# The end of a feed-forward stage in another order, and a fifth landing buffer for weights

## What is computed

```python
def first_block(x, ...):
    for l in range(DEPTH):                                  # DEPTH = 2
        x = layer_norm(ALPHA * x + 0.5 * swiglu(x, ffn1_w13[l], ffn1_w2[l]), ...)
        m = mixer(x, w_in[l], ...)
        x = layer_norm(ALPHA * x + m, ...)
        x = layer_norm(ALPHA * x + 0.5 * swiglu(x, ffn2_w13[l], ffn2_w2[l]), ...)

def second_block(x, ...):
    for layer in range(DEPTH):
        h = swiglu_2(rms_norm(x, g[0]), ffn_w_in[layer, 0], ffn_w_out[layer, 0])
        x = x + 0.5 * rms_norm(h, g[1])
        h = token_mixer(rms_norm(x, g[2]), mix_w_in[layer], ...)
        x = x + rms_norm(h, g[3])
        h = swiglu_2(rms_norm(x, g[4]), ffn_w_in[layer, 1], ffn_w_out[layer, 1])
        x = x + 0.5 * rms_norm(h, g[5])

def swiglu(x, w13, w2):
    a, b = jnp.split(x @ w13, 2, axis=-1)                   # 2816 hidden features each
    return (jax.nn.silu(a) * b) @ w2
```

## Time and profile before

| | us |
|---|---|
| median of 3 runs (lowest, highest) | 2115.8 (2115.5, 2116.16) |
| profiled execution, its time | 2114.63 |
| its span in the profile | 2112.9 |
| TensorE busy with matmuls | 2090.4 (99%) |
| VectorE busy | 1686.0 (80%) |
| ScalarE busy | 1081.8 (51%) |
| POOL busy | 84.5 (4%) |
| SyncE's transfers, share of 16 DMA engines | 57.6% |
| issue to landing, median, by kind of weight load | 3.2 to 4.1 |
| TensorE's granted clock, mean | 0.999 |

### The profile page before, as it was taken

One profiled execution on the slowest core, in us unless ns is written; L12 is line 12 of the kernel. 1 busy time (PEld: TensorE's weight loads), 2 busy tenths in 40 slices (PEclk: granted clock), 3 DMA queues, 4 the chain that ended last, 5 costly groups with the idle time before them and its releaser, 6 DMA issues.

```text
span 2112.9 us, 28855 instructions
## 1 busy us (share of the span) xinstructions
PE 2090.4 (99%) x10552; PEld 1774.3 (84%) x10552; DVE 1686.0 (80%) x3158; ACT 1081.8 (51%) x1568; POOL 84.5 (4%) x127
## 2 busy tenths in 40 slices
PE   8999999999999999999999999999999999999998
PEld 7887999888788799988878887988888888888886
DVE  6888766888888877778888887779888888678886
ACT  6445554544544455444454446575445445665543
POOL 0000010000000000000000001010000000101000
PEclk9999999999999999999999999999999999999999
DMA  7765755566566574656646666346665765645663
GB/s 249 234 194 169 224 166 157 188 217 191 174 218 196 174 234 139 190 168 224 196 153 213 215 191 196 125 136 207 214 195 171 220 196 163 185 140 165 214 191 98
DMA packets 314368, 395.56 MB, mean 187 GB/s; under 512 B 17972, under 2 KB 272212, under 8 KB 313972
## 3 DMA queue, kind: packets, MB, share of 16 engines
q1 hardware_dynamic: 309120, 375.52, 57.6%
q0 software_dynamic: 4944, 18.14, 2.7%
q10 hardware_dynamic: 164, 0.06, 0.0%
HBM read 392.59 MB, written 1.06 MB: 186 GB/s over the span
## 4 chain that ended last, share of the span: by engine, by line
PE 93%; DVE 4%; ACT 1%; issue 1%; DMA 1%; POOL 0%; SPq 0%; DVEq 0%; POOLq 0%; ACTq 0%
PE bank L309 25%; PE bank L311 25%; PE bank L310 25%; PE bank L303 4%; PE bank L304 4%; PE bank L305 4%; DVE w_lo L293 1%; PE bank L478 1%; DVE hidden L464 1%; PE bank L1442 1%; PE bank L1463 1%; PE bank L972 1%; DMA stage<-in_mix_w_in 1%; PE bank L1534 1%; ACT w_hi L286 0%
## 5 line engine op out<-in xcount | busy, mean ns | idle before, releaser
L286 ACT ACTIVATE w_hi<-stage 128x1024 fp32r<-128x1024 f32 x711 | 747.1, 1058 | 635.0 <-PE bank L311 527.2
L293 DVE TENSOR_TENSOR w_lo<-stage,w_hi 128x1024 fp32r<-128x1024 f32 x711 | 865.2, 1224 | 213.7 <-ACT w_hi L286 206.9
L309 PE MATMUL bank<-w_hi,xt_hi 128*128 128x512 f32 x1760 | 692.9, 394 | 0.6 <-DVE xt_lo L816 0.4
L311 PE MATMUL bank<-w_hi,xt_lo 128*128 128x512 f32 x1760 | 686.7, 390 | 0.0
L310 PE MATMUL bank<-w_lo,xt_hi 128*128 128x512 f32 x1760 | 686.5, 390 | 0.0
L464 DVE STREAM_TRANSPOSE hidden<-hidden 32x128 f32<-32x128 f32 (+1 forms) x1376 | 391.7, 285 | 21.3
L309 PEld LDWEIGHTS bank<-w_hi,xt_hi 128*128 128x128 f32 x1760 | 331.0, 188 | 69.6 <-issue 1.2
L311 PEld LDWEIGHTS bank<-w_hi,xt_lo 128*128 128x128 f32 x1760 | 330.9, 188 | 68.8
L310 PEld LDWEIGHTS bank<-w_lo,xt_hi 128*128 128x128 f32 x1760 | 331.1, 188 | 66.5
L309 PE MATMUL bank<-w_hi,mt_hi 128*128 128x512 f32 x768 | 304.1, 396 | 6.7 <-DVE mt_lo L546 6.7
L311 PE MATMUL bank<-w_hi,mt_lo 128*128 128x512 f32 x768 | 299.8, 390 | 0.0
(11 more groups left out here) (275 smaller groups left out, 1384.2 us busy)
## 6 DMA issues: line engine op xcount, KB each, us to landing
stage<-in_ffn_w SPq DMA_DIRECT2D x352, 256.0 KB, 3.2
stage<-in_ffn_w_in SPq DMA_DIRECT2D x352, 256.0 KB, 3.2
stage<-in_ffn_w SPq DMA_DIRECT2D x88, 512.0 KB, 3.7
stage<-in_ffn_w_out SPq DMA_DIRECT2D x88, 512.0 KB, 3.7
stage<-in_w_in SPq DMA_DIRECT2D x80, 512.0 KB, 4.1
stage<-in_mix_w_in SPq DMA_DIRECT2D x56, 512.0 KB, 3.9
stage<-in_w_out SPq DMA_DIRECT2D x16, 512.0 KB, 4.1
stage<-in_mix_w_out SPq DMA_DIRECT2D x16, 512.0 KB, 3.4
```

What stands on the lines that cost most here:

```text
L286: act.activation(w_hi[:, u % RING, :], stage[:, u % STAGED, :], ACT.Copy).then_inc(S["hi_ready"], 1)
L293: dve.tensor_tensor(w_lo[:, u % RING, :], stage[:, u % STAGED, :], f32(w_hi[:, u % RING, :]), ALU.subtract).then_inc(S["lo_ready"], 1)
L309: pe.matmul(o, m_hi, hi, start=first, stop=False)
L311: return pe.matmul(o, m_lo, hi, start=False, stop=last)
```

## The change

Three things are changed. The number of landing buffers goes from 4 to 5, so that a load waits for the low part of the unit five back. The memory for it comes from two row tables that are given up: `ones8` and `g_neg1` now lie in `gm`, and POOL writes the ones anew in each of the second block's mixers; the steps of the lower bounds count on `tables_out` in place of a semaphore of their own. And the end of each feed-forward stage has another order on VectorE, in the first block on ScalarE too.

```diff
-STAGED = 4
+STAGED = 5
...
-    margins=6, mixrows2=32, wg_in=16, wg_hi=1, wg_lo=1,
+    margins=7, mixrows2=32, wg_in=16, wg_hi=1, wg_lo=1,
...
-        g_neg1 = sb("g_neg1", [2 * H, T])
-        ones8 = sb("ones8", [2 * H, T])
...
+        ones8 = gm[0:2 * H, 1, 0:T]
-        g_neg_rows = hidden_flat[0:2 * H, 768:768 + T], g_neg1[:, :]
+        g_neg_rows = hidden_flat[0:2 * H, 768:768 + T], gm[0:2 * H, 0, 0:T]
...
+            if s < BLOCK2:
+                act_silu(act, s, 1, STEPS - 1)
             act_norm_sq(act, s, 0)
-            act_silu(act, s, 1, STEPS - 1)
+            if s >= BLOCK2:
+                act_silu(act, s, 1, STEPS - 1)
             act_h(act, s, 1, STEPS - 1)
...
-            dve_norm_start(dve, s, 0)
-            dve_gate(dve, s, 1, STEPS - 1)
+            dve_norm_start(dve, s, 0, lambda: dve_gate(dve, s, 1, STEPS - 1))
             dve_norm_var(dve, s, 0)
+            dve_h(dve, s, 1, STEPS - 1)
             dve_norm_x(dve, s, 0)
-            dve_h(dve, s, 1, STEPS - 1)
...
-        def dve_norm_start(dve, s, t):
+        def dve_norm_start(dve, s, t, between=lambda: None):
+
             wait_acc(dve, s, t)
...
                    .then_inc(S["ln_mean"], 1)
+                between()
                 dve.wait_ge(S["ln_mean"], ln_at(s, t))
...
                     dve.tensor_tensor(r[:, t, c], acc[:, t, c], rows[:, 0, c], ALU.mult).then_inc(S["post_scaled"], 1)
+                between()
...
-            act.wait_ge(S["lb_step"], 3)
-            act.activation(lb_tmp[:, 3:5, :], lb_tmp[:, 1:3, :], ACT.Exp).then_inc(S["lb_step"], 1)
+            act.wait_ge(S["tables_out"], 6)
+            act.activation(lb_tmp[:, 3:5, :], lb_tmp[:, 1:3, :], ACT.Exp).then_inc(S["tables_out"], 1)
...
                 dve.wait_ge(S["g_rows"], at("g_rows", L))
+                dve.wait_ge(S["margins"], at("margins", L, 1))
...
+            pool.memset(ones8, 1.0).then_inc(S["margins"], 1)
             pool.memset(xp[:, :, 0:2], 0.0).then_inc(S["margins"], 1)
...
-            pool.memset(ones8[:, :], 1.0).then_inc(S["ones_set"], 1)
...
-            dve.wait_ge(S["ones_set"], 2)
```

More of the change, by code:

```diff
@@ L857, in dve_tables @@
             mx = lb_tmp[:, 0, :]
-            dve.tensor_tensor(mx, lbr_tab[:, 0, :], lbr_tab[:, 1, :], ALU.max).then_inc(S["lb_step"], 1)
-            dve.wait_ge(S["lb_step"], 1)
+            dve.tensor_tensor(mx, lbr_tab[:, 0, :], lbr_tab[:, 1, :], ALU.max).then_inc(S["tables_out"], 1)
+            dve.wait_ge(S["tables_out"], 4)
             for l in range(2):
-                dve.tensor_tensor(lb_tmp[:, 1 + l, :], lbr_tab[:, l, :], mx, ALU.subtract).then_inc(S["lb_step"], 1)
+                dve.tensor_tensor(lb_tmp[:, 1 + l, :], lbr_tab[:, l, :], mx, ALU.subtract).then_inc(S["tables_out"], 1)
         def dve_lower_bounds(dve):
             mx, e = lb_tmp[:, 0, :], lb_tmp[:, 3:5, :]
[L865 to L874, removed]
+            dve.wait_ge(S["tables_out"], 7)
+            dve.tensor_tensor(lb_tmp[:, 5, :], e[:, 0, :], e[:, 1, :], ALU.add).then_inc(S["tables_out"], 1)
+            dve.wait_ge(S["tables_out"], 8)
+            dve.reciprocal(mx, lb_tmp[:, 5, :]).then_inc(S["tables_out"], 1)
+            dve.wait_ge(S["tables_out"], 9)
+            dve.tensor_tensor(lb_tab[:, 1, :], e[:, 1, :], mx, ALU.mult).then_inc(S["tables_out"], 1)
+            dve.memset(lb_tab[:, 0, :], 0.0).then_inc(S["tables_out"], 1)
+            dve.wait_ge(S["tables_out"], 11)
+            dve.tensor_scalar(om_tab, lb_tab, -1.0, 1.0, ALU.mult, ALU.add).then_inc(S["tables_out"], 1)
+            dve.wait_ge(S["tables_out"], 12)
         def w_cols(w, c0, n, k0=0, nk=KD):
@@ L1792, in gate_rows @@
                 dve.wait_ge(S["g_rows"], at("g_rows", L))
+                dve.wait_ge(S["margins"], at("margins", L, 1))
                 rev = (slice(None), slice(None, None, -1))
-                dve.tensor_tensor_scan(g_cum_rows[0], ones8[:, :], g_lf_row, 0.0, ALU.mult, ALU.add)\
+                dve.tensor_tensor_scan(g_cum_rows[0], ones8, g_lf_row, 0.0, ALU.mult, ALU.add)\
                    .then_inc(S["g_scan"], 1)
-                dve.tensor_tensor_scan(g_cum_rows[1][rev], ones8[:, :], g_lf_row[rev], 0.0, ALU.mult, ALU.add)\
+                dve.tensor_tensor_scan(g_cum_rows[1][rev], ones8, g_lf_row[rev], 0.0, ALU.mult, ALU.add)\
                    .then_inc(S["g_scan"], 1)
@@ L1808, in gate_bounds @@
                     dve.wait_ge(S["g_scan"], at("g_scan", L, d + 3))
-                    dve.tensor_tensor_scan(o, ones8[:, :], a, -1e30, ALU.mult, ALU.max).then_inc(S["g_scan"], 1)
+                    dve.tensor_tensor_scan(o, ones8, a, -1e30, ALU.mult, ALU.max).then_inc(S["g_scan"], 1)
                 for d in range(2):
@@ L1981, in pool_mix2 @@
             pool.memset(va[:, :, :, P:P + 1], 1.0).then_inc(S["margins"], 1)
-            pool.wait_ge(S["margins"], at("margins", L, 3))
+            pool.wait_ge(S["margins"], at("margins", L, 4))
             pool.memset(q_odd_parts[1][0:64], 0.0).then_inc(S["margins"], 1)
-            pool.wait_ge(S["margins"], at("margins", L, 4))
+            pool.wait_ge(S["margins"], at("margins", L, 5))
             pool.wait_ge(S["x_turned"], xt_at(s, 1, 1))
             pool.memset(aqk_t[64:P, 0:4, :], 0.0).then_inc(S["margins"], 1)
-            pool.wait_ge(S["margins"], at("margins", L, 5))
+            pool.wait_ge(S["margins"], at("margins", L, 6))
             pool.wait_ge(S["rot"], at("rot", L))
```

4 lines of the change are left out of this document (2 added, 2 removed).

## The result

The changed kernel takes 2111.8 us (median of 16 runs, 2111.19 to 2112.9), the kernel before 2115.74 (16 runs, 2114.86 to 2116.42): ratio 0.9981, interval 0.9975 to 0.9987. That is 3.9 us less, and the forecast of 2111.7 is met within 0.1. The profiled execution took 2112.07 (span 2110.3).

What follows compares the result with a forecast made beforehand. TensorE, busy 99%, was taken as the bound, losing time mainly at eight feed-forward ends. Terms 2.9 - 0.1 + 1.1 + 0.2 = 4.1 us off the median 2115.8 gave 2111.7, range 2109.0 to 2114.5.

Steps and rivals of the forecast that it cites:

- The place of the loss: TensorE's stalls at the ends of all eight feed-forward stages, 10.7 us, most of what there is to win.
- Block 1, 3 x 0.93: Three first-block ends gain 0.93 us each from the new order, after a new wait for xt_lo.
- 1.64: TensorE's loss in us at one first-block feed-forward end: 0.65 at the transposes plus 0.99 at the low part.
- 0.71: Part in us of a first-block end's 1.64 that turns into a new wait for xt_lo at the next opening.
- The end before block 2, +0.07: Fourth first-block end, where VectorE's chain counts: normalisation 0.27 later, low part's 0.34 gone from behind it, gain 0.07 us.
- The other three of block 2, -0.03 each: Second-block ends but the last: VectorE's chain 0.03 us later each, -0.1 together; the wait only moves.
- The last end, 1.13: Program's last feed-forward end: no next stage, so the low part's wait goes and 1.13 us come off.
- The order in sum: The reordering's terms in the forecast sum: 2.9 in block 1, -0.1 in block 2, 1.1 at the last end.
- The fifth buffer, 0.2: Earlier loads save only TensorE's 0.2 us wait for the copy at line 1618.
- the upper bound that was given with it: Fifth buffer worth at most 1 us, if small waits at the program's start go too.
- the first rival: Buffer worth more: a twentieth of ScalarE's 51 us of landing waits counts, 2.5 us, giving 2109.2; chance 0.12.
- POOL beside the low part: POOL's rstd running beside VectorE's low part on their shared port: counted as nothing, bound 2.9 us at seven ends.

Runs made afterwards that it cites:

- experiment 3: Kernel before with SiLU and gate product moved first in block 1, low part still last, four buffers: 2120.25 us, ratio 1.0018.
- experiment 4: Kernel before with only the low part moved ahead of the normalisation, SiLU still late, four buffers: 2113.12 us, ratio 0.9986.
- Experiment 5: Changed kernel with tile 0's xt_lo put between VectorE's two weight subtractions: 2107.73 us, ratio 0.996 to the kernel before.
- experiment 1: Kernel before with the new order alone, four landing buffers and the old tables: 2112.85 us, ratio 0.9986.
- experiment 12: Kernel before profiled a second time without any edit: 2116.12 us.
- experiment 11: The kernel of experiment 3 profiled a second time: 2121.25 us.
- experiment 8: Experiment 1 with the lower bounds' work 18 units later, four buffers: 2112.02 us, ratio 0.998 to the kernel before.
- experiment 6: Experiment 5 with one weight subtraction behind tile 1's normalisation at three block-1 openings: 2106.98 us, ratio 0.9958 to the kernel before.
- experiment 9: Experiment 6 with the lower bounds moved as in experiment 8, five buffers: 2107.06 us, ratio 0.9957 to the kernel before.

## Why the prediction was right, and where it was not

- *The place of the loss: right.* Eight ends, two stalls each in block 1, one in block 2. With the low part put first the waits for it vanish at all eight, and experiments 3 and 4 take the two moves apart.
- *Block 1, 3 x 0.93: measured 0.88, 0.77 and 0.82.* The path was the forecast one (normalisation, two halves, two subtractions, xt_lo), each step within 0.07. The sum left out that the matmul behind a wait is followed late: at the opening 194.69, then 195.03, 0.34 apart instead of 0.23. The old stalls had such steps too (0.31 behind the one at 191.23), and these go with them. So at the first end 1.77 is gone where 1.64 was counted, and 0.90 comes back where 0.71 was counted: 0.87 against 0.93. Experiment 5 shows that this wait is the subtractions' doing.
- *The end before block 2, +0.07: measured -0.07. The other three of block 2, -0.03 each: measured -0.15, -0.11 and -0.16.* The mis-sized term is the step from the normalisation to the product with the gain, which the earlier trace rows gave as 1.20 because the low part stood between them. In the new order the product follows at once and waits for the normalisation's end, 1.31 behind its start:

```profile
1275.55 1.28 DVE L780 SCALAR_TENSOR_TENSOR x<-r,rstd,x 128x1024 f32<-128x1024 f32 x1
1276.86 1.29 DVE L805 TENSOR_TENSOR xh<-x,rows 128x512 f32<-128x512 f32 x2
...
1280.34 1.28 DVE L820 TENSOR_TENSOR xt_lo<-bank,xt_hi 128x512 fp32r<-128x512 f32 x2
...
1281.08 0.50 PE L308 MATMUL bank<-w_hi,xt_hi 128*128 128x512 f32 x1 [0.83 <-DVE xt_lo L820]
```

- *The last end, 1.13: measured 1.24.* Nothing comes back here, and the stall goes together with the late restart behind it (0.31 instead of 0.23).
- *The order in sum: forecast 3.9, in the profiles 2.47 - 0.07 - 0.42 + 1.24 = 3.2, in medians 3.0.*
- *The fifth buffer, 0.2: measured 1.0.* This term was wrong: the measurement is the upper bound that was given with it, and not for the reason given there. The 0.2 was read as one wait for line 1618, which the buffer removes. Right in kind: in the changed kernel it is gone. But it comes and goes without the buffer as well (not in the lists of experiments 1, 3, 4 and 12; 0.5 us in 11, 0.8 in 8). The larger piece, the stall near 60 us, is the shape that the first rival described (a late landing that makes ScalarE's other work late), at one place and not as a twentieth of everything. That it is there with four buffers and not with five is shown by 4 of 6 profiles against none of 7; the way from the landing at 43 us to the stall at 60 is read from one timeline and not shown by an experiment. It could not be read from the earlier trace rows, since that one execution had landed in time; its 1.2 us under the median was the only hint, and the forecast named it and did not ask what it stood for.
- *So the total was right partly by luck:* the order gave 0.7 to 0.9 less than forecast, the buffer 0.8 more. The forecast had put 0.12 on a worth of 2.5 us for the buffer, and no chance of its own on one near 1.
- *POOL beside the low part: right at nothing.* POOL's power took 0.56 in the changed kernel's row, as in the first of the earlier trace rows; POOL waited 7.5 us for the broadcast of the gate rows where it had been 7.05, and its masks were still done 1.6 us before ScalarE's use of them.

## What to carry to other kernels

When a stall is removed by changing an engine's order, follow that engine to its next consumer and price the new wait there: here about half of each 1.64 in the first block came back at the wait for xt_lo, and reordering that consumer too (experiments 5 and 6) was worth more than the first change. A half move can be worse than none, since it can join two short stalls into a long one (experiment 3). And one profile shows one execution: where it lies a microsecond beside the median, a second profile of the same kernel says what is missing from it.

## What the runs showed of the hardware

- Behind a single stall of TensorE of 1.97 to 2.08 us the clock fell to 1.2 GHz (granted 0.50) in three of the eight block-1 ends of two profiles (experiments 3 and 11), 0.3 to 0.7 us after TensorE had started again, and stayed there for 3.4 us each time while TensorE was busy. It did not fall behind any stall of 1.2 us and less in the two profiles of the kernel before, nor behind the waits of 1.4 us at block 2's opening in experiments 5, 6 and 9.
- A matmul of 512 columns that follows one which waited starts 0.30 to 0.34 behind it, where 0.23 is the usual step: 0.31 behind the waits for the low part, short (0.8) and long (1.8 to 1.9), up to 0.34 behind those for xt_lo.
- Landings differ between executions of the same kernel: the conversion near 42 us waited 0.16 us for its landing in one execution of the kernel before and 1.68 in the other.
